# Gated delta rule of two layers: from chunks of six heads to pairs of heads over all chunks

## The reference, cut to what matters

```
S <- exp(g_t) * S
u_t = beta_t * (v_t - k_t S)
S <- S + outer(k_t, u_t)
o_t = q_t S
```

## Time and profile before

| | us |
|---|---|
| median of 3 runs (lowest, highest) | 3831.06 (3827.61, 3834.22) |
| the profiled execution's own time | 3828.58 |
| its span, first to last instruction | 3826.8 |
| mean granted TensorE clock, of full speed | 0.949 |
| TensorE busy, share of the span | 91% |
| VectorE, ScalarE, GpSimd busy | 47%, 34%, 11% |

### The profile page before, as it was taken

The page is one execution under the profiler, slowest core; times in us unless marked ns, Lnnn a source line. Parts: engine busy times, 40 slices in busy tenths (PEclk is TensorE's granted clock), DMA queues, the critical chain, the costliest instruction groups (busy, mean ns, idle before and its releaser), DMA issues. The chain is left out here.

```text
span 3826.8 us, 46458 instructions
## 1 busy us (share of the span) xinstructions
PE 3475.4 (91%) x19317; PEld 2705.3 (71%) x19317; DVE 1780.1 (47%) x2762; ACT 1308.2 (34%) x2038; POOL 420.6 (11%) x351
## 2 busy tenths in 40 slices
PE   5989897999999789998897988999989988899998
PEld 4877765788777567886665756788766665577886
DVE  4775465443332534332544454444444444554534
ACT  2332353223232332322422353333333134533333
POOL 0001000120000101100023000221001310013100
PEclk7999998999999899999899999999989989999999
DMA  6651215333221032331301103232122020213231
GB/s 228 199 175 45 78 34 187 118 124 110 90 75 55 1 132 69 105 109 35 99 18 27 37 1 110 87 100 101 66 76 61 2 63 1 88 55 110 77 110 50
DMA packets 230575, 316.69 MB, mean 83 GB/s; under 512 B 13133, under 2 KB 167606, under 8 KB 229086
## 3 DMA queue, kind: packets, MB, share of 16 engines
q1 hardware_dynamic: 230366, 313.72, 24.9%
HBM read 311.04 MB, written 6.85 MB: 83 GB/s over the span
## 5 line engine op out<-in xcount | busy, mean ns | idle before, releaser
L493 PE MATMUL out<-h_lo,w_hi 128*128 128x512 f32 x2608 | 1043.1, 400 | 52.1 <-DVE w_lo L484 47.8
L494 PE MATMUL out<-h_hi,w_hi 128*128 128x512 f32 x2608 | 1022.2, 392 | 0.0
L495 PE MATMUL out<-h_hi,w_lo 128*128 128x512 f32 x2608 | 1021.6, 392 | 0.0
L484 DVE TENSOR_TENSOR w_lo<-ring,w_hi 128x1024 fp32r<-128x1024 f32 (+2 forms) x459 | 560.7, 1227 | 980.0 <-ACT w_hi L479 974.9
L479 ACT ACTIVATE w_hi<-ring 128x1024 fp32r<-128x1024 f32 (+2 forms) x459 | 469.2, 1027 | 1152.9 <-PE out L495 1061.1
L493 PEld LDWEIGHTS out<-h_lo,w_hi 128*128 128x128 f32 x2608 | 494.0, 189 | 178.1 <-issue 60.4
L494 PEld LDWEIGHTS out<-h_hi,w_hi 128*128 128x128 f32 x2608 | 493.8, 189 | 111.9 <-issue 11.0
L495 PEld LDWEIGHTS out<-h_hi,w_lo 128*128 128x128 f32 x2608 | 493.6, 189 | 103.9
L493 PE MATMUL item_banks<-h_lo,w_hi 128*128 128x512 f32 (+1 forms) x632 | 289.4, 458 | 14.3 <-DVE w_lo L484 5.1
L494 PE MATMUL item_banks<-h_hi,w_hi 128*128 128x512 f32 (+1 forms) x632 | 255.1, 404 | 0.0
L495 PE MATMUL item_banks<-h_hi,w_lo 128*128 128x512 f32 (+1 forms) x632 | 254.8, 403 | 0.0
(11 more groups left out here) (499 smaller groups left out, 4635.8 us busy)
## 6 DMA issues: line engine op xcount, KB each, us to landing
ring<-in_mlp_w SPq DMA_DIRECT2D x30, 2048.0 KB, 8.5
ring<-in_w_up SPq DMA_DIRECT2D x44, 1024.0 KB, 7.4
tiles<-in_mod_w SPq DMA_DIRECT2D x80, 512.0 KB, 4.6
ring<-in_e_w_in SPq DMA_DIRECT2D x48, 512.0 KB, 4.1
ring<-in_w_down SPq DMA_DIRECT2D x10, 2048.0 KB, 7.7
ring<-in_w_in SPq DMA_DIRECT2D x16, 1024.0 KB, 5.2
ring<-in_o_w_in SPq DMA_DIRECT2D x7, 2048.0 KB, 7.9
tiles<-in_mod_w SPq DMA_DIRECT2D x8, 1024.0 KB, 8.8
```

The costliest lines, as they stand in the source:

```text
L484: return nc.vector.tensor_tensor(lo.bitcast(F32R), x, hi, ALU.subtract)
L493: nc.tensor.matmul(out, wh, xl, start=start, stop=False, **kw)
L494: nc.tensor.matmul(out, wh, xh, start=False, stop=False, **kw)
L495: return nc.tensor.matmul(out, wl, xh, start=False, stop=stop, **kw)
```

## The change

- `delta_lane` goes by pairs of heads (one tile of q, k and v, t = 0, 1, 2) over all four chunks at once: 512 columns where 384 were, eight half-chunks in the recurrence. Three programs for each pair are merged on TensorE by due times: `norms`, `inverse` and `recurrence`. For pair t, `PAIRS` gives their due times: norms 53.0, 86.5, 123.5; inverse 59.5, 96.5, 133.5; recurrence 95.5, 132.5, 169.5.
- The recurrence keeps all eight states (`hist`), and has of its own the banks that were the norms' (`stat_banks`). The inter part is computed for all half-chunks at its end.
- `key_norm_lane` is gone, with its load of the table set by hand. Its steps stand in `delta_lane`.
- The projection's items come in the order q0 k0 v0, q1 k1 v1, q2 k2 v2, nq, kv, gz. The three SiLUs of a pair are due together, 2.0 behind the pair's third item. All items from the fourth conv item on are 7.0 long. Each load of weights is two transfers of 128 columns.
- The rotation is due at 155.3 over 13.5, between the recurrences of pairs 1 and 2; pair 2's recurrence waits until it has left the banks.
- Two constant tables become one of 640 columns in place of 1024; three attention buffers move to the region that uses them.

The diff, cut to its core:

```diff
+        tile_of = [part * GDN_T + t for t in range(GDN_T) for part in range(3)]
+        cols_of = [W_GDN + j * P for j in tile_of] + [W_NQ + j * P for j in range(NSA_T)] + [W_KC, W_KC + P, W_KC + 2 * P, W_KW]
+        cols_of += [W_GDN + (3 * GDN_T + j) * P for j in range(GDN_T)]
...
+        BEGIN, PAIR, BESIDE = 18.0, 37.0, 7.0
         at = BEGIN
-        for item in items:
-            item.begin, item.length = at, 3.2 if item.load == 0 else 5.6 if at < DELTA else 9.4
+        for m, item in enumerate(items):
+            item.begin, item.length = at, 3.2 if item.load == 0 else 5.6 if m < TC + 3 else BESIDE
             at += item.length
+        for n in range(3 * GDN_T):
+            last = items[TC + 3 * (n // 3) + 2]
+            items[TC + n].silu_at = last.begin + last.length + 2.0 + 0.7 * (n % 3)
+        pairs_at = []
+        for t in range(GDN_T):
+            here = items[TC + 2].silu_at + 8.5 + PAIR * t
+            pairs_at.append((here - 6.5 if t == 0 else here - 10.0, here, here + 36.0))
+        ROTARY = pairs_at[1][2] + 22.8
...
+            turned_away = rotary_lane(k, r, r.lane(ROTARY, 13.5), [nq[:, j, :] for j in range(NSA_T)] + [kv[:, j, :] for j in (0, 2, 3)],
+                                      [kc2, vc2, ks2, kw2], kv_turned[:, 0:2, :], stat_banks,
+                                      [(freed[0], (last_kv + 1) // 2), (freed[1], last_kv // 2)], [(pass_out, 2 * (GDN_T - 1))])
+            delta_lane(k, r, r.lane(0.0, 1.0), qkv, (g, beta, beta_eg, to_end), mixT, scratch, ends, hist, kv_turned, delta_banks, stat_banks,
+                       steps_ready, silu_done, pass_out, turned_away, pairs_at)
...
-        nc.scalar.preload_act_table_set(EXP_LN_SET)
...
+                steps += [(end, 2, m), (end + 3.0 if item.silu_at is None else item.silu_at, 3, m)]
...
+            yield at + 3.2
+            pool.wait_ge(exp_done, 2 * t + 1)
+            pool.wait_ge(prepared, LEVELS * t + 4)
+            nc.gpsimd.tensor_tensor(low, low, mask_beta, ALU.mult).then_inc(masked, 1)
+            pool.wait_ge(tb_done, t + 1)
+            nc.gpsimd.tensor_tensor(heads(attns[t % 2]), heads(attns[t % 2]), mask("upto_c"), ALU.mult).then_inc(masked, 1)
+            yield at + 7.0
+            pool.wait_ge(low_t_done, 2 * t + 2)
+            pool.wait_ge(decay_done, 2 * t + 2)
+            pool.wait_ge(run_done, 2 * t + 2)
+            pool.wait_ge(masked, 2 * t + 1)
+            for n in range(LEVELS):
+                nc.gpsimd.tensor_tensor(heads(parts[n]), heads(low_t), mask(f"level_{n + 1}"), ALU.mult).then_inc(part_done, 1)
+                yield at + 8.0 + 1.5 * n
+            pool.wait_ge(run_out, t + 1)
+            pool.wait_ge(kq_done, t + 1)
+            nc.gpsimd.tensor_tensor(qkv[:, t, :], qkv[:, t, :], run, ALU.mult).then_inc(qrun_done, 1)
+            if t + 1 < T:
+                for m in range(LEVELS):
+                    yield at + 14.5 + 4.4 * m
+                    pool.wait_ge(y_done, 2 * LEVELS * t + 2 * (m + 1))
+                    prepare(t + 1, m)
...
+        order = []
+        for t, (norm_at, at, run_at) in enumerate(PAIRS):
+            order += [(norm_at, norms, t), (at, inverse, t), (run_at, recurrence, t)]
+        threads = [[begin, n, program(pe, t, begin)] for n, (begin, program, t) in enumerate(order)]
+        while threads:
+            thread = min(threads, key=lambda x: x[:2])
+            yield thread[0]
+            time = next(thread[2], None)
+            if time is None:
+                threads.remove(thread)
+            else:
+                thread[0] = time
...
+    def norms(pe, t, at):
+        pe.wait_ge(steps_ready, 1)
+        if t >= 2:
+            pe.wait_ge(pass_out, 2 * (t - 1))
+        elif t:
+            pe.wait_ge(log_done, 2 * t)
+        for j in range(2):
+            yield at + 0.7 + 0.9 * j
+            pe.wait_ge(squared, 2 * t + j + 1)
+            nc.tensor.matmul(run_banks[:, j, :], k.at["ones_64"], sq[:, j, :], start=True, stop=True).then_inc(stat_done, 1)
...
+        for n in range(LEVELS):
+            for b in range(2):
+                yield at + 11.0 + 4.4 * n + 1.1 * b
+                if n == b == 0:
+                    pe.wait_ge(low_done, 2 * t + 2)
+                pe.wait_ge(part_done, LEVELS * t + n + 1)
+                pe.wait_ge(inv_done, 2 * (LEVELS + 1) * t + 2 * n + b + 1)
+                for c in range(TC):
+                    for i in range(2):
+                        rows = rows_of(i)
+                        last = nc.tensor.matmul((B0, B1)[b][rows, c * HD:(c + 1) * HD], of_head(parts[n], b, c)[rows, :],
+                                                of_head(inv, b, c)[rows, :], start=True, stop=True)
+                last.then_inc(y_done, 1)
+            for b in range(2):
+                yield at + 12.9 + 4.4 * n + 1.1 * b
+                pe.wait_ge(y_out, 2 * LEVELS * t + 2 * n + b + 1)
...
+    def recurrence(pe, t, at):
+        pe.wait_ge(zeroed, 1)
+        pe.wait_ge(uw_out, 2 * t + 2)
+        if t + 1 < T:
+            pe.wait_ge(log_done, 2 * (t + 2))
+        else:
+            for wait in turned_away:
+                pe.wait_ge(*wait)
+        k_end = qkv[:, 2 * T + t, :]
+        for s in range(STEPS):
+            c, i = s // 2, s % 2
+            rows = rows_of(i)
+            if s:
+                yield at + 2.6 * s
+                pe.wait_ge(state_done, (STEPS - 1) * t + s)
+                for b in range(2):
+                    last = nc.tensor.matmul((R0, R1)[b][rows, 0:HD], w_t[rows_of(b), (i * TC + c) * HD:(i * TC + c + 1) * HD], hist[rows_of(b), s, :],
+                                            start=True, stop=True)
+                last.then_inc(new_done, 1)
+            if s < STEPS - 1:
+                yield at + 2.6 * s + 1.3
+                if s:
+                    pe.wait_ge(new_out, (STEPS - 1) * t + s)
+                for b in range(2):
+                    last = nc.tensor.matmul(R0[rows_of(b), HD:2 * HD], of_head(k_end, b, c)[rows, :], of_head(u, b, c)[rows, :], start=True, stop=True)
+                last.then_inc(grow_done, 1)
...
+            steps += [(norm_at + 1.3 + 1.3 * j, "norm", t, j) for j in range(2)]
+            steps += [(at + 1.5, "decay", t, 0), (at + 4.3, "run", t, 0), (at + 34.8, "uw", t, 0), (run_at + 2.6 * (STEPS - 1) + 1.6, "inter", t, 0)]
+            steps += [(at + 12.0 + 4.4 * n + 1.1 * b, "y", t, 2 * n + b) for n in range(LEVELS) for b in range(2)]
+        return sorted(steps, key=lambda x: x[0])
...
+            if what == "norm":
+                act.wait_ge(stat_done, 2 * t + n + 1)
+                if t:
+                    act.wait_ge(normed, 2 * t)
+                inverse_root(k, act, rstd[:, n, :], rstd[:, n, :], run_banks[:, n, :], 1.0, log_done, 2 * t + n + 1).then_inc(rstd_done, 1)
...
+            steps += [(norm_at + 0.6 * j, "square", t, j) for j in range(2)]
+            steps += [(norm_at + 3.0 + 1.3 * j, "norm", t, j) for j in range(2)]
+            steps += [(at + 2.0, "rows", t, 0), (at + 4.2, "both", t, 0), (at + 6.0, "low", t, 0), (at + 8.5, "attn", t, 0)]
+            steps += [(at + 14.0 + 4.4 * n + 1.1 * b, "inv", t, 2 * n + b) for n in range(LEVELS) for b in range(2)]
+            steps += [(run_at + 2.6 * s + 0.7, "new", t, s) for s in range(1, STEPS)]
+            steps += [(run_at + 2.6 * s + 2.0, "state", t, s) for s in range(STEPS - 1)]
+            steps.append((run_at + 2.6 * (STEPS - 1) + 3.6, "pass", t, 0))
+        return sorted(steps, key=lambda x: x[0])
```

More of the change, by code:

```diff
@@ L748, in _ @@
             if item.kind == "conv":
-                steps += [(end, 2, m), (end + 3.0, 3, m)]
+                steps += [(end, 2, m), (end + 3.0 if item.silu_at is None else item.silu_at, 3, m)]
             elif owner(m) == "act":
@@ L3208, in _ @@
-    @lane.tensor
-    def _(pe):
-        for j in range(N):
-            yield (j + 0.1) / (N + 1)
-            pe.wait_ge(squared, j + 1)
-            if j >= 2:
-                pe.wait_ge(rstd_done, j - 1)
-            nc.tensor.matmul(stat[:, j % 2, :], k.at["ones_64"], sq[:, j % 2, :], start=True, stop=True).then_inc(stat_done, 1)
-    @lane.scalar
-    def _(act):
-        nc.scalar.preload_act_table_set(EXP_LN_SET)
-        for j in range(N):
-            yield (j + 0.5) / (N + 1)
-            act.wait_ge(stat_done, j + 1)
-            if j >= 2:
-                act.wait_ge(normed, j - 1)
-            inverse_root(k, act, rstd[:, j % 2, :], rstd[:, j % 2, :], stat[:, j % 2, :], 1.0, log_done, j + 1).then_inc(rstd_done, 1)
@@ L3633, in second_mixer @@
+        ranges += [[(col, P) for col in cols_of[n:n + 2]] for n in range(0, len(cols_of), 2)]
         items = [Item("rows", 0, 0, 2 * P + 30, by_token[:, c:c + 1, :], (c,)) for c in range(TC)]
-        items += [Item("conv", 1 + j // 2, j % 2 * P, P, qkv[:, j, :], tile=j) for j in range(3 * GDN_T)]
-        items += [Item("feat", 1 + j // 2, j % 2 * P, P, gz[:, j - 3 * GDN_T, :]) for j in range(3 * GDN_T, 4 * GDN_T)]
```

(30 more changed lines are left out.)

619 lines of the change are left out of this document (281 added, 338 removed).

## The result

The changed kernel takes 3852.24 us (median of 5 runs, 3849.58 to 3856.41), the kernel before 3831.06: ratio 1.0054, interval 1.0041 to 1.0068. It is slower, as forecast, by 21 us where 13 were forecast (3844). The profiled execution took 3852.24, with a span of 3850.5.

What follows compares the result with a forecast made beforehand. TensorE, busy 91% of the span, was taken as the bound. Per layer 226.4 + 30.4 = 256.8 us against 250.5, 6.3 more, 12.6 for two layers: 3844 us forecast, range 3806 to 3870.

Steps and rivals of the forecast that it cites:

- Fed stretch: Part of each layer's mixing region where the input projection runs beside the delta rule: 192.7 us before, 226.4 forecast.
- Waits and clock: TensorE's waits and slow-clock loss while projection steps run: 22.9 us per layer forecast, against 20.5 before.
- Seams: Delta runs between projection steps, each costing 0.34 us beyond its own work: 89 instead of 55, 11.6 us more per layer.
- Norms: ScalarE's key norms with added table loads delay copies of y that TensorE awaits: 7.5 us per layer, bounds 0 to 15.
- State behind the low block: Recurrence's state update queues behind a 5.4 us VectorE block; TensorE waits 3.7 us at pairs 1 and 2: 7.4.
- Tail: End of each mixing region, with no projection left: 57.8 us before, 30.4 forecast, 27.4 less.
- The 14 hops: Last recurrence, seven steps of two hops between TensorE and VectorE: 12.5 us, bounds 10 to 18.
- the closing part: From the last recurrence to the attention region's first product, with 32 closing products and a copy: 4.3 us, 1.95 before.
- The sum: Whole mixing region per layer: 256.8 us against 250.5, so 6.3 more, 12.6 for two layers.
- The waits fold into one another: Faster rival, at pairs 1 and 2: waits hidden and small groups cheaper, 12.8 us gained per layer, 3805; chance 0.27.
- The sets go together: Rival: one ScalarE table load serves Ln and Exp, 7 us of norm wait and 1.6 of clock go, 3826; chance 0.05.
- The recurrence paces TensorE: Slower rival: 26 recurrence hops beside the projection lose 0.5 us each, the last recurrence 5, giving 3880; chance 0.1.

Runs made afterwards that it cites:

- the kernel with the three edits: Changed kernel with the Ln/Exp table set loaded, VectorE's low block in three parts and output-gate items due late: 3821.07 us, 0.9968 of before.
- the tables run: Changed kernel with the table set of Ln and Exp loaded, 7 table loads per mixing region instead of 17: 3836.5 us, 1.001 of before.

## Why the prediction was right, and where it was off

**The direction** and the mechanism held: the tail's gain is real, and the fed stretch takes it back. Term by term, for layer 0:

*Fed stretch:* 226.4 forecast, 224.1 found, and 225.9 in layer 1. Waits and clock, 22.9 by the forecast, are some 21 if the other terms hold at the forecast's prices, with one product of the rotation less (see the tail); 15.1 of them are idle time.

*Seams:* 89 forecast, 90 counted, and 53 in place of the forecast's 55 for the kernel before. The 37 that came in are 8 to 12 us a region at 0.22 to 0.33 each, and TensorE's busy time grew by 9.1 and 13.6. At 0.34 they were 30.3, and the small groups of the recurrence, for which no row stood, cost that too. But removing 34 of all kinds gave 0.27 each, and 35 in the kernel with the three edits 0.22. So 0.34 reads right in the timeline, and is worth less by removal; why is not shown.

*Norms:* 7.5 forecast, as idle time. Found: 0.75, 2.65 and 1.37, 4.8 in all; the two large ones were put at 2.1 and 3.3, so pair 2's was too high and pair 1's a little low. 17 loads were forecast and found. Taken out, they were worth 7.5 us a region with the slow products behind the waits. The forecast's 7.5 was idle time alone and had the clock as a term beside it, so that the two figures agree is luck: the idle time was over-sized by 2.7.

*State behind the low block:* 3.7 forecast twice, 3.67 and 5.29 found. The forecast priced TensorE's side and the block, but not what VectorE had still to do for the projection when the block came due: at pair 2 L558 and L483, 1.9 us.

*Tail:* 30.4 forecast, 34.1 found. The term that was mis-sized is the one ahead of the recurrence: from the last projection product to its first product it was 10.6 + 3.0 = 13.6, and took 16.7 (2069.45 to 2086.19). All of it lies in levels and rotation, 13.9 up to L3390 in place of 10.6. Seven products of the rotation were left where six were counted (three of L3611, four of L3619), 0.9 us. And the forecast had no seam in the tail, but the rotation's products stand singly between block products: one product (two instructions) takes 1.06 (2070.39 to 2071.45), while two in a row take 1.92 (2081.39 to 2083.31), so a further one is 0.86 and the switch 0.20, and with 0.14 on the block products it is the fed stretch's 0.34. Six such switches are 2.0. The 14 hops were 12.5 and took 11.9 (2086.19 to 2098.07), the closing part 4.3 and took 5.5.

*The sum:* 6.3 us a region forecast; 7.7 and 12.3 found. In layer 0 two errors cancel, 2.3 too much in the fed stretch and 3.7 too little in the tail, so that its sum came so near is in part luck. In layer 1 the forecast took 250.5 for the region of before, though it was 247.1 by the earlier trace rows, and in the changed kernel layer 1's is no shorter than layer 0's: 3.2 us of the 6.0 by which this region missed. The 4.3 us behind layer 1's region, which the change doesn't touch, lie within the scatter of that stretch over the twelve kernels.

**The rivals.** "The waits fold into one another" fell: not one of the four waits was hidden. But its terms were the right list: with the norms' loads and the block's length removed by hand, and gate items moved into the tail, the waits shrank and the kernel came out under the old one, at 3821.07. "The sets go together" fell by the trace of the changed kernel, and the tables run showed its price: 7.5 us a region where 8.6 was forecast. "The recurrence paces TensorE" fell: a hop in the fed stretch is covered by steps, and its only long waits are those behind the low block.

**What the change was worth with its side effects mended.** With its order kept and four of them mended (loads by hand, the block in three, gate items in the tail, steps in twos), pairs of heads over all chunks gain 0.7% on the kernel before. Of these mends the old order had the first already, and the last one harms it. The block in three and the gate items in the tail were not tried on it, although it has waits behind its own low block (2.87 us in the earlier trace rows) and a tail of 58 us. So the 0.7% compares a mended new order with an old one that was not mended, and what the new order is worth by itself is not shown. What the runs do show is that the 21 us of loss can be taken back, and more, without giving up the new order.

## What to carry to other kernels

When work moves from an idle tail into a stretch that is full, its products cost the same there; the gain is only the idle time and the slow clock of the tail, so subtract every added switch and every wait before hoping for it. Before shifting a step on a queue, list the long blocks already on that queue, the projection's own among them, and cut a block of several us into entries that short, critical operations can pass. An interruption between two kinds of products can pay where it covers a dependency and is lost where something else covers it already, so its granularity has to be tried anew after each reordering.

## What the runs showed that was not expected

Waits cost more than their length: 4.4 us of idle time removed in each region shortened it by 7.5. The tail, filled with projection steps, ran at a granted clock of 1.00 in place of 0.76, and TensorE's busy time in the region became 4.6 us shorter, though idle time fell by only 1.5.

The same edit, projection steps in twos, was worth -19.4 us in one order and +8.0 in the other.

The price of a seam is 0.33 us by the timeline, for groups of 4 and of 16 alike, and 0.22 to 0.27 by removal.
